# Rebuilding the residual input on VectorE inside the first merge loop instead of on GpSimd

## The reference, cut to what matters

```
xn = rmsnorm(x, norm_mix)
z  = xn @ w_in                                  # u, v, B, C, h, gate_A, gate_B
a     = gelu(u) * spatial_gate(layernorm(gelu(v)))
bconv = B * causal_conv3(C * h)
m = sigmoid(gate_A) * (a @ w_pa) + sigmoid(gate_B) * (bconv @ w_pb)
x = x + m @ w_o                                 # the residual addition
x = x + (silu(rmsnorm(x) @ w_gate) * (rmsnorm(x) @ w_up)) @ w_down
y = rmsnorm(x, norm_final)
```

## Time and profile before

| what | value |
|---|---|
| three runs | 945.57, 945.96, 948.23 us; median 945.96 us |
| the profiled execution's own time | 944.17 us |
| its span, first to last instruction | 942.4 us |
| what lies around the span | 944.17 - 942.4 = 1.77 us |
| mean granted clock of TensorE | 0.993 |
| busy: PE, DVE, ACT, POOL | 922.2, 512.6, 259.4, 62.9 us |
| mean DMA rate | 89 GB/s |

### The profile page before, as it was taken

The page is one execution under the profiler, slowest core; times in us unless marked ns, Lnnn a source line. Parts: engine busy times, 40 slices in busy tenths (PEclk is TensorE's granted clock), DMA queues, the critical chain, the costliest instruction groups (busy, mean ns, idle before and its releaser), DMA issues.

```text
span 942.4 us, 17750 instructions
## 1 busy us (share of the span) xinstructions
PE 922.2 (98%) x7273; PEld 917.0 (97%) x7273; DVE 512.6 (54%) x923; ACT 259.4 (28%) x378; POOL 62.9 (7%) x64
## 2 busy tenths in 40 slices
PE   6999999999998999999999999999999999999995
PEld 6999999999998999999999999999999999999995
DVE  4567777666566333355578655555533355555452
ACT  7333332223233333222211211222212122112331
POOL 0000010000004000000024200000000000000330
PEclk8999999999999999999999999999999999999998
DMA  9221232221222222222222222222223422221312
GB/s 282 94 73 63 90 96 90 86 73 64 89 89 70 72 85 88 90 89 89 89 90 90 90 90 90 89 89 67 67 84 116 134 82 80 78 65 48 90 48 95
DMA packets 90230, 83.50 MB, mean 89 GB/s; under 512 B 1612, under 2 KB 88756, under 8 KB 90196
## 3 DMA queue, kind: packets, MB, share of 16 engines
q1 hardware_dynamic: 90196, 83.03, 28.0%
HBM read 80.65 MB, written 2.38 MB: 88 GB/s over the span
## 4 chain that ended last, share of the span: by engine, by line
PE 97%; DMA 1%; issue 0%; SPq 0%; DVE 0%; ACT 0%; ACTq 0%; DVEq 0%
PE ps_main L425 32%; PE ps_main L423 31%; PE ps_main L424 31%; DMA tok<-in_x_prompt_dram 1%; PE ps_g L544 1%; PE ps_g L455 0%; PE ps_t L455 0%; PE ps_g L545 0%; PE ps_g L464 0%; PE ps_t L529 0%; PE ps_t L448 0%; SPq L325 0%; PE ps_main L630 0%; ACT tok L808 0%; ACTq L109 0%
## 5 line engine op out<-in xcount | busy, mean ns | idle before, releaser
L423 PE MATMUL ps_main<-act_hi,w_hi 128*128 128x272 f32 x2336 | 676.5, 290 | 3.2 <-DVE sig L861 3.2
L425 PE MATMUL ps_main<-act_hi,w_lo 128*128 128x272 f32 x2336 | 677.5, 290 | 0.0
L424 PE MATMUL ps_main<-act_lo,w_hi 128*128 128x272 f32 x2336 | 672.8, 288 | 0.0
L423 PEld LDWEIGHTS ps_main<-act_hi,w_hi 128*128 128x128 f32 x2336 | 440.8, 189 | 4.3 <-DVE sig L861 3.4
L424 PEld LDWEIGHTS ps_main<-act_lo,w_hi 128*128 128x128 f32 x2336 | 441.4, 189 | 0.2 <-issue 0.2
L425 PEld LDWEIGHTS ps_main<-act_hi,w_lo 128*128 128x128 f32 x2336 | 440.1, 188 | 0.0
L645 ACT CAST w_hi<-w_raw 128x2048 fp32r<-128x2048 f32 x50 | 95.3, 1906 | 283.6 <-PE ps_main L425 283.5
L848 DVE TENSOR_TENSOR w_lo<-w_raw,w_hi 128x2048 fp32r<-128x2048 f32 x50 | 128.0, 2559 | 48.2 <-ACT w_hi L645 48.0
L650 ACT ACTIVATE w_hi<-w_raw,g_cols 128x256 fp32r<-128x256 f32 x224 | 92.5, 496 | 97.8 <-PE ps_main L425 97.4
L854 DVE SCALAR_TENSOR_TENSOR w_lo<-w_raw,g_cols,w_hi 128x256 fp32r<-128x256 f32 x224 | 91.4, 480 | 47.6 <-ACT w_hi L650 47.3
L1153 DVE TENSOR_TENSOR gate_sb<-ps_main,r_all 128x544 f32<-128x544 f32 x22 | 16.0, 725 | 73.6 <-PE ps_main L425 73.3
(11 more groups left out here) (151 smaller groups left out, 364.2 us busy)
## 6 DMA issues: line engine op xcount, KB each, us to landing
w_raw<-in_w_in_dram SPq DMA_DIRECT2D x27, 1024.0 KB, 5.1
w_raw<-in_w_gate_dram SPq DMA_DIRECT2D x11, 1024.0 KB, 5.3
w_raw<-in_w_up_dram SPq DMA_DIRECT2D x11, 1024.0 KB, 5.3
w_raw<-in_w_down_dram SPq DMA_DIRECT2D x8, 768.0 KB, 4.7
w_raw<-in_w_down_dram SPq DMA_DIRECT2D x8, 640.0 KB, 4.3
w_raw<-in_w_pa_dram SPq DMA_DIRECT2D x4, 1024.0 KB, 4.9
w_raw<-in_w_pb_dram SPq DMA_DIRECT2D x4, 1024.0 KB, 5.0
w_raw<-in_w_o_dram SPq DMA_DIRECT2D x4, 1024.0 KB, 5.0
```

Of the source, the lines that this page charges most:

```text
L423: pe.matmul(out, whi, xhi, start=(k == 0), stop=False)
L424: pe.matmul(out, whi, xlo, start=False, stop=False)
L425: last = pe.matmul(out, wlo, xhi, start=False, stop=(k == blocks - 1))
```

## The change

The GpSimd instruction that fills resid is taken out, with its two waits. DVE fills resid itself: in each of the four passes of the first merge loop (merge_a), after the two evictions of the gate unit and before it splits the next w_lo, it adds the high and low parts of two blocks, 2j and 2j + 1. So DVE issues eight tensor_tensor instructions of 128x544, each counting `resid_ready` up by one. DVE waits for `b_ready` ahead of the loop, beside the waits it had for `staged` and `a_ready`, and ahead of stage out it waits for `resid_ready` to be 8 where it waited for 1.

```diff
             p = ph["merge_a"]
             dve.wait_ge(staged, KD)
             dve.wait_ge(a_ready, KD)
+            dve.wait_ge(b_ready, KD)
             with dve.Fori(0, 4) as j:
                 take_times_r(p, j, 0, 0, sig[:, 0, :], r_x)
                 take_times_r(p, j, 0, 1, sig[:, 1, :], r_x)
+                for i in range(2):
+                    dve.tensor_tensor(resid[:, 2 * j + i, :], fbits(act_hi[:, XN + 2 * j + i, :]),
+                                      fbits(act_lo[:, XN + 2 * j + i, :]), ALU.add).then_inc(resid_ready, 1)
                 split_lo(p, j, 1, norm=True)
...
             p = ph["out"]
-            dve.wait_ge(resid_ready, 1)
+            dve.wait_ge(resid_ready, KD)
...
-            pool.wait_ge(a_ready, KD)
-            pool.wait_ge(b_ready, KD)
-            pool.tensor_tensor(resid[:], fbits(act_hi[:, XN:XN + KD, :]), fbits(act_lo[:, XN:XN + KD, :]),
-                               ALU.add).then_inc(resid_ready, 1)
```

## The result

The changed kernel takes 940.99 us in the median of seven runs (939.5 to 941.49), the kernel before 945.96 us (943.72 to 948.23, seven runs too). The ratio is 0.9948, with an interval of 0.9936 to 0.9961: about 4.9 us faster, between 3.7 and 6.1.

The account below looks back on a forecast made before the run. PE's matmul stream was taken as the bound, with one avoidable hole: -3.47 (hole) + 0 (adds) + 0 (waits) on 945.96 gave 942.5 us. The forecast's own range was 941.4 to 944.4, the wider range 940.2 to 944.6.

Parts of the forecast that it names:

- The hole is the bound part: Behind the start, PE's matmul stream has one hole: a 3.2 us wait for DVE's eviction after the first gate unit.
- L848 stands still behind GpSimd's sum: First w_pa unit's w_lo on DVE takes 11.04 us instead of 2.29, standing still until GpSimd's sum over resid finishes.
- C: Rival: GpSimd doesn't cause the stretched L848, or another wait takes its place; hole stays, 945.96 us; 7 in 100.
- The hole costs 3.47 us: Two PE steps after the first gate unit take 3.72 us where 0.25 would do; all 3.47 us come back.
- Nothing takes over the wait: Without GpSimd's sum, the first eviction and w_lo are ready before PE needs them, so no new wait appears.
- The 5.2 us of spare: First gate tile's eviction is done near 286.7, and PE wants it at 291.9: 5.2 us to spare.
- The adds cost nothing: In each merge_a pass, 1.46 us of adds fit DVE's 3.92 us idle time before L854: cost zero.
- The threshold of 7.3 us: In merge_a, PE notices the adds only when two take more than 3.92 + 3.4 = 7.3 us per pass.
- D: Rival: adds in DVE's queue between evictions and L854 slow all four passes; 948.8 us with 4.5 us adds; 3 in 100.
- The waits that were moved cost nothing: DVE's waits for b_ready and a_ready before the loop and resid_ready before stage out each cost nothing.
- The sum, -3.47 on the median: Whole kernel: -3.47 + 0 + 0 on the three runs' median of 945.96 us gives 942.5 us, 0.37%.
- B: Rival: the hole also drops PE's clock behind it, costing 1.9 us more; gain 5.3 us, time 940.6; 12 in 100.

Follow-up runs that it names:

- e2: Kernel before, with GpSimd's whole sum over resid started only once the first w_pa unit's L848 is written: 940.72 us, ratio 0.9954.
- e3: Kernel before, with GpSimd's sum at its old place cut into eight one-block instructions: 941.23 us, ratio 0.9955 to the kernel before.
- e6: Changed kernel with the eight adds replaced by one DVE sum in front of the first w_pa unit's L848: 940.77 us, ratio 0.9953 to the kernel before.
- e10: Changed kernel with one DVE sum in front of L848, then four of the eight blocks summed again: 941.97 us, ratio 0.9969 to the kernel before.
- e11: Changed kernel with 8 adds in each pass instead of 2 (6 repeats without use): 940.69 us, ratio 0.9960 to the kernel before.
- e8: Changed kernel with 14 adds in each pass instead of 2 (12 repeats without use): 958.81 us, ratio 1.015 to the kernel before.
- e5: Kernel before, unedited, traced a second time: 947.61 us in one run.
- e9: Kernel before, unedited, traced a third time: 944.43 us in one run.
- e7: Changed kernel with the adds replaced by one whole DVE sum in front of L848, issued twice: 945.27 us, ratio 0.9999 to the kernel before.

## Why the prediction was right, point by point

*The hole is the bound part.* Right. No other wait of PE behind the start is left, and the tails of the seven traces without a hole agree to 0.1 us.

*L848 stands still behind GpSimd's sum.* Right, and shown: with the same sum 3.1 us later (e2) L848 takes 2.29 us, and with it cut into pieces (e3) 2.85, and neither leaves a hole. C falls.

*The hole costs 3.47 us.* Right for an execution whose clock holds: 3.38 in the traced pair.

*Nothing takes over the wait.* Right. The 5.2 us of spare for the first eviction hold 4.7 us of DVE work (e6), and 7.1 us make a hole of 0.8 (e10). Both started in the 0.75 us for which DVE waits for ACT.

*The adds cost nothing.* Right. They take 1.35 us a pass (0.716 us each; I took 1.46) in an idle time of 4.0. The threshold of 7.3 us lies where it was put: 5.9 us are free (e11), and 10.47 us cost 3.24 in e8's third pass, which lost nothing but its hole, so 7.2 are free. D falls.

*The waits that were moved cost nothing.* No run takes them apart; the trace shows none of them.

*The sum, -3.47 on the median.* This is the term that was mis-sized: the clock behind the hole, put at nothing. The one trace I had showed the clock at 1.00 behind the hole, and I gave B 12 in 100 and put nothing of it into the sum. That trace was of an execution without the loss; two more traces of the same kernel have it, 1.56 and 2.57 us. The hint was there: the three runs were slower than the profiled one by 1.4 us and more, and I called it a difference that no row explains. The change removes the hole and with it this loss, so by the tails the gain is 3.4, 4.9 or 6.0 us against the three traced executions of the kernel before. By the ratios it is 4.9 us, and 3.8 to 5.0 in the five later comparisons of kernels without a hole. So B, which I had as a rival of the forecast, is part of the truth: the hole alone and the hole with the clock are two kinds of execution of one kernel. B's own gain of 5.3 us is nearer to what was measured than the forecast's 3.47, and that 940.99 us lies within the stated range is owed to B, for which the range was drawn below 941.4. The prediction cites the Trainium skill, "TensorE: Matmul & The Clock Gate", section "HAM oscillation — how this bites in real kernels", for idle gaps of PE that put its clock back to half speed: the traces of e5 and e9 agree with it (0.50 behind the hole), the first trace does not (1.00).

## What to carry to other kernels

When a GpSimd instruction that reads SBUF and a DVE instruction with two SBUF inputs overlap, look at which starts first: here the other waited to its end (11.04 us instead of 2.29), so one long GpSimd instruction "off the critical path" can open a hole on PE. Starting it after the urgent DVE instruction, or cutting it into pieces, gave as much here as moving the work to DVE. And price a hole in PE's stream with the clock it may cost behind it; one trace in which the clock held says little, while runs that are slower than the profiled one ask for a second.

## What the runs showed of the hardware that I had not expected

The same hole of 3.2 us is followed by no slow stretch, one of 3.3 us or one of 5.6 us, from one execution to the next; the one of 3.07 us in e7 was followed by one too, the one of 0.80 us (e10) by none in its trace. It differs even within one execution: of the four holes of 3.0 us in e8, the first two were followed by a slow stretch and the last two by none. In e9 the clock falls only when PE has been at work again for 1.3 us. What decides between the cases stays open.
